# Gated delta heads on one Trainium2 core: norm factors folded into columns, 16x16 blocks inverted on VectorE

## The reference, cut to what matters

```python
qkv = jax.nn.silu(dwconv(pa[..., :3 * BR_W], conv_w))
q = l2norm(heads(qkv[..., :BR_W], H_A)) * (DK_A ** -0.5)
k = l2norm(heads(qkv[..., BR_W:2 * BR_W], H_A))
...
kb = k * beta
lower = jnp.where(strict, jnp.einsum('bhnid,bhnjd->bhnij', kb, k) * decay, 0.0)
rhs = jnp.concatenate([v * beta, kb * jnp.exp(gc)[..., None]], axis=-1)
sol = lax.linalg.triangular_solve(lower + jnp.eye(CHUNK, dtype=jnp.float32), rhs,
                                  left_side=True, lower=True, unit_diagonal=True)
...
o = rmsnorm(o_f + rev(o_b), norm_g)
y = merge_heads(o) * jax.nn.silu(z.astype(jnp.float32))
```

## Time and profile before

| | before |
|---|---|
| three runs, us | 2526.24, 2527.37, 2527.37 |
| the profiled execution, us | 2526.02 |
| its span, us | 2524.5 |
| mean granted TensorE clock | 0.997 |
| TensorE products busy, us | 2446.4 |
| VectorE / ScalarE / GpSimd busy, us | 1332.0 / 992.5 / 320.8 |

### The profile page before, as it was taken

The page is one execution under the profiler, slowest core; times in us unless marked ns, Lnnn a source line. Parts: engine busy times, 40 slices in busy tenths (PEclk is TensorE's granted clock), DMA queues, the critical chain, the costliest instruction groups (busy, mean ns, idle before and its releaser), DMA issues. The chain is left out here.

```text
span 2524.5 us, 56135 instructions
## 1 busy us (share of the span) xinstructions
PE 2446.4 (97%) x23072; PEld 2330.3 (92%) x23072; DVE 1332.0 (53%) x2347; ACT 992.5 (39%) x1908; POOL 320.8 (13%) x398
## 2 busy tenths in 40 slices
PE   7999999999999999999999999999999999999998
PEld 5889889999999999989988898899999999999898
DVE  5565653677333434663565656537773344356644
ACT  4555532333234424452365455323332353255422
POOL 1322201000012101110012222100000110011000
PEclk9999999999999999999999999999999999999999
DMA  7101114111234233124221110231113332222122
GB/s 270 46 31 40 31 37 149 43 43 51 101 106 106 81 108 99 57 63 147 76 92 46 31 40 23 69 133 34 51 50 87 88 91 83 77 68 82 55 99 84
DMA packets 55734, 193.86 MB, mean 77 GB/s; under 512 B 9080, under 2 KB 9246, under 8 KB 55376
## 3 DMA queue, kind: packets, MB, share of 16 engines
q1 hardware_dynamic: 40352, 147.34, 17.4%
q0 software_dynamic: 15152, 43.24, 6.3%
HBM read 177.97 MB, written 8.39 MB: 74 GB/s over the span
## 5 line engine op out<-in xcount | busy, mean ns | idle before, releaser
L734 PE MATMUL proj<-h_hi,w_hi 128*128 128x320 f32 x3072 | 739.5, 321 | 4.3 <-DVE h_lo L2171 2.9
L734 PE MATMUL proj<-h_lo,w_hi 128*128 128x320 f32 x3072 | 702.0, 309 | 0.0
L734 PE MATMUL proj<-h_hi,w_lo 128*128 128x320 f32 x3072 | 698.7, 309 | 1.3 <-issue 1.3
L2171 DVE TENSOR_TENSOR w_lo<-raw,w_hi 128x1024 fp32r<-128x1024 f32 x232 | 287.8, 1241 | 480.4 <-ACT w_hi L1573 479.6
L734 PEld LDWEIGHTS proj<-h_hi,w_hi 128*128 128x128 f32 x3072 | 504.1, 189 | 20.3 <-issue 5.9
L734 PEld LDWEIGHTS proj<-h_lo,w_hi 128*128 128x128 f32 x3072 | 514.8, 188 | 0.0
L734 PEld LDWEIGHTS proj<-h_hi,w_lo 128*128 128x128 f32 x3072 | 513.0, 188 | 1.6 <-issue 1.6
L734 PE MATMUL mix<-area 64*64 64x64 f32 (+6 forms) x8176 | 470.8, 236 | 11.8 <-issue 4.5
L734 PEld LDWEIGHTS mix<-area 64*64 64x64 f32 (+4 forms) x8176 | 405.0, 140 | 61.7 <-issue 36.5
L1573 ACT ACTIVATE w_hi<-raw 128x1024 fp32r<-128x1024 f32 x232 | 245.8, 1060 | 532.7 <-PE proj L734 329.7
L1573 ACT ACTIVATE area<-mix 128x256 f32<-128x256 f32 (+8 forms) x462 | 189.3, 433 | 632.9 <-PE mix L734 510.1
(11 more groups left out here) (304 smaller groups left out, 2653.7 us busy)
## 6 DMA issues: line engine op xcount, KB each, us to landing
raw<-in_w_in SPq DMA_DIRECT2D x128, 512.0 KB, 3.5
raw<-in_w_mb SPq DMA_DIRECT2D x96, 512.0 KB, 3.5
raw<-in_w_mod POOLq DMA_DIRECT2D x32, 512.0 KB, 4.7
area<-in_bias POOLq DMA_DIRECT2D x64, 128.0 KB, 4.6
raw<-in_w_out SPq DMA_DIRECT2D x16, 512.0 KB, 3.5
out_x<-area SPq DMA_DIRECT2D x10, 512.0 KB, 2.6
merged<-in_w_mod SPq DMA_DIRECT2D x8, 512.0 KB, 11.3
area<-area POOLq DMA_DIRECT2D x64, 64.0 KB, 1.9
```

The lines of the kernel that those rows point to most:

```text
L734: return T.matmul(out, l, r, start=start, stop=stop)
L2171: return V.tensor_tensor(out, a_, b_, op)
```

## The change

- **Norms.** Keys and queries stay unnormalised. Silu writes straight into `kq`, the operand of gram and scan. ScalarE squares it (`A_squared`), and ten products with one column of ones in front unit 3 give the sums; GpSimd takes the powers and multiplies them into the columns of beta (`A_front`); the queries' factor goes into the output norm. The 15 transposes of `kqn` and of q are gone, the front has 10 units with 20 transposes. Rv is now made by ScalarE.
- **Small blocks.** Levels 0 to 3 are gone. VectorE cuts the 16x16 diagonal blocks out (`A_decays`, `A_blocks`); five DMAs (three by SP, two by GpSimd) bring them to 40 partitions with a whole block in each; VectorE eliminates pivot by pivot, 28 small operations (`A_scaled`, `A_pivots`, `A_inverse`); five DMAs bring the inverses back, and VectorE and ScalarE spread them into X and Y (`A_spread`). Of the levels, one in halves, mid and last are left.
- **Order.** Front units 0 to 2 (the decays) of the next head stand among the first eighths of a head, units 3 to 9 in the scan; all engines' orders are rewritten. Blocks come right behind step 0 of the scan, pivots 1 to 3 behind step 3, pivots 4 to 8 and 9 to 14 before and behind w_lo of the next head's fourth unit.

```diff
@@ SP
+                def relay(h):
+                    sp.wait_ge(A_own.sem, A_own.at(layer, 3 * h + 2))
...
+                    for t in range(SP_TILES):
+                        blocks_in(sp, t, A_relay)
+                    sp.wait_ge(A_own.sem, A_own.at(layer, 3 * h + 3))
...
+                    for t in range(SP_TILES):
+                        inverses_back(sp, t, A_relay)
@@ GpSimd, A_front
+                    pool.wait_ge(A_fev.sem, A_fev.at(layer, FRONT * h + 4))
...
+                    P.tensor_tensor(roots, roots, neg_half[:, 0:10], ALU.pow)
...
+                    pt(A_head(1, h), A_head(1, h), both(rn_k(h))).then_inc(A_rn.sem, A_rn.step)
...
+                    pool.wait_ge(A_own.sem, A_own.at(layer, 3 * h + 1))
...
+                    pt(dec, decT, beta_sq.unsqueeze(3).to_broadcast([128, 2, TILES, 128])).then_inc(A_dm.sem, A_dm.step)
+                    pool.wait_ge(A_own.sem, A_own.at(layer, 3 * h + 2))
...
+                    for t in range(SP_TILES, TILES):
+                        blocks_in(pool, t, A_relay_pool)
@@ TensorE, A_front and A_levels
+                    elif u == 3:
+                        tr(o(0), kq[:, 0, tile(4)])
+                        for i in range(2):
+                            for t in range(TILES):
+                                last = mm(o(1)[:, 5 * i + t:5 * i + t + 1], A_c[:, i, tile(t)], ones[:, 0:1])
...
+                    fill(0, 1)
+                    if h < HEADS - 1:
+                        A_front(h + 1, 0)
+                        A_front(h + 1, 1)
+                    fill(1, 5)
+                    if h < HEADS - 1:
+                        A_front(h + 1, 2)
+                    fill(5, 17)
+                    A_level_q(h)
+                    fill(17, 18)
+                    A_level_d(h)
+                    if h:
+                        pe.wait_ge(proj_taken.sem, proj_taken.at(layer, u0 + 2))
+                        A_out(h - 1, psum_a[(u0 + 1) % 2])
+                    fill(18, 20)
+                    A_mid_q(h)
+                    fill(20, 21)
+                    A_mid_d(h)
+                    fill(21, 22)
+                    A_last_q(h)
+                    fill(22, 23)
+                    A_last_d(h)
+                    fill(23, 24)
@@ VectorE
+                def A_pivots(first, end):
+                    for p in range(first, end):
+                        n = 15 - p
+                        below = Z[:, p + 1:16, :, 0:p]
+                        tmp = Z_tmp[:, 0:2 * n * p].rearrange("q (i d c) -> q i d c", i=n, d=2)
+                        mul(tmp, Z[:, p + 1:16, :, p:p + 1].to_broadcast([40, n, 2, p]), Z[:, p, :, 0:p].unsqueeze(1).to_broadcast([40, n, 2, p]))
+                        fence()
+                        tt(below, below, tmp, ALU.subtract)
+                        fence()
...
                         if n == 0:
-                            A_squares(h + 1)
+                            A_blocks(h + 1)
                         elif n == 1:
-                            A_norms(h + 1)
-                        elif n == 2:
-                            A_normed(h + 1)
-                        elif n == 4:
                             A_lower(h + 1)
+                        elif n == 3:
+                            A_scaled(h + 1)
+                            A_pivots(1, 4)
```

More of the change, by code:

```diff
@@ L608, in _ @@
                 A_store(HEADS - 1)
[L609 removed]
+                A_o_root(HEADS - 1)
                 A_store_done(HEADS - 1)
@@ L1128, in part @@
                                 A_front(h + 1, u)
-                        if h < HEADS - 2:
+                        if h < HEADS - 2 and first < end:
+                            if h and first == 0:
+                                pe.wait_ge(A_ox.sem, A_ox.at(layer, h))
                             eighths(0, 4 * h + 8, first, end)
@@ L1133, in last_part @@
                         if h == HEADS - 1:
+                            if first <= 24 < end:
+                                pe.wait_ge(A_ox.sem, A_ox.at(layer, h))
                             eighths(0, 16, first, end)
@@ L2389, in update @@
+                def update(h):
+                    masks = [over(level[:, i, :].unsqueeze(1), TILES, 64) for i in range(2)]
                     for d in range(2):
-                        dve.wait_ge(A_d.sem, A_d.at(layer, e + (d + 1)))
+                        dve.wait_ge(A_d.sem, A_d.at(layer, 4 * h + (d + 1)))
                         held(dve)
-                        V.copy_predicated(X[:, d], masks[d], cols(1024 * d, 64) if lv else Q[:, d])
+                        V.copy_predicated(X[:, d], masks[d], cols(1024 * d, 64))
```

565 lines of the change are left out of this document (296 added, 269 removed).

## The result

| | before | the change |
|---|---|---|
| median, us | 2527.4 | 2546.3 (2540.2 to 2548.9) |
| ratio, 95% interval | | 1.007 (1.0057 to 1.0082) |
| profiled execution, us | 2526.0 | 2540.2 |
| its span, us | 2524.5 | 2538.7 |
| mean granted clock | 0.997 | 0.976 |

The forecast was 2531 with a range of 2498 to 2562. The time is 15 over it, 19 over before. The profiled execution of the change is the fastest of its four: the others took 2544.4 to 2548.9 us at a mean granted clock of 0.970 or 0.971.

What follows compares the result with a forecast made beforehand. TensorE, busy 97%, was taken to bound the kernel. Removed work and old pauses less new waits, with the layers' starts and end, gave −7.9; clock falls +12.8: 2526.0 − 7.9 + 12.8 = 2531 us, range 2498 to 2562.

Steps and rivals of the forecast that it cites:

- removed work turns into pauses: Leading case, whole kernel: work taken off TensorE returns as pauses of about the same length; 2515 to 2546 us, chance 0.45.
- What leaves TensorE: TensorE, branch A: delta groups of the dropped levels go, 52.5 us a layer, less 2.2 net for the changed front.
- The column products: Front, TensorE: ten one-column products a head, twenty instructions at 0.11 us each, +2.2 us; bounds nothing to 0.22 each.
- The new gate: Before the first kept level: TensorE waits for the 16x16 inverses to be spread, 6.6 to 6.9 us a head, 26.7 a layer.
- The relay back: Transfer returning the inverses before the spread: 1.9 us, bounds 1 and 6, covered by VectorE's convolution.
- Other new waits: TensorE per layer: output's transposes 1.9 × 3, mid and last levels 0.7 × 4, scan's start 6.2, third scan step 9.4 us.
- The scan's start: Scan start in three heads: TensorE waits for the third convolution, split, w_lo, value silu, gate and copy; 6.2 us.
- The layers' starts: Start of branch A: uncovered front work and waits for decay columns and square, +6.1 us in layer 0, +3.2 in layer 1.
- The third scan step: Scan: VectorE's blocks, slowed by meeting GpSimd's multiply, make this step 3.0 to 3.4 us late in three heads; 9.4 a layer.
- The clock: Behind the gate: one fall to half clock a head, about 3 us long, 1.6 lost, 8 × 1.6 = +12.8 us.
- B: Rival, faster: GpSimd's multiply misses the blocks, −18.8, and the clock stays full at the gate, −12.8; 2499 us, chance 0.32.
- C: Rival, slower: pivots at 0.5 us each lengthen the gate, +19, with second clock falls; 2556 or 2562 us, chance 0.23.

## Why the prediction was right

The sign of its sum (+4.9), its range and its leading case, *removed work turns into pauses*, came out; its point was 15 low (9 low against the profiled execution, 2540.2). The mechanism held for the gate; the number is near in part by luck, as the last steps show. By its own steps:

- **What leaves TensorE**, −100.6 for both layers: −100.0. The column products at 0.11 each: 2.29 for 20, so the row of 20 columns was the right one. Head 3's 14.05 should read 14.2 by its own terms, which changes nothing. The section "Wait — 56ns, not 53.3ns?" of the Trainium skill's page "TensorE: Matmul & The Clock Gate" gave an estimate of 1.2 for the twenty. The trace's 2.29 is above the floors stated there, so they are not what bounds here; weights of 128x128 come with each product, and 118 columns took nearly the same 2.39.
- **The new gate**, 6.6 a head in heads 0 to 2 and 6.9 in head 3: 6.0, 5.3, 5.5 and 5.7, 22.5 for 26.7 in layer 0, and 20.9 in layer 1. The chain's links were all there, pivots at 0.30. The chain ended at 24.5 (122.7 less the first eighth at 98.2) for 23.7. TensorE's idle time in heads 0 to 2 is less than forecast since the eighth and the level's first half, which stand between the pauses, ran at the low clock and filled part of them (3.2 us in head 0). In head 3 nothing stands between, and what made its 5.7 out of 6.9 was not looked into. The relay back was priced at 1.9; it took 4.5 in head 3, where the spread waits for it.
- **Other new waits.** The output's transposes, 1.9 × 3: 1.93 in three heads. The mid and last levels, 0.7 × 4: 3.0 in layer 0, with 1.10 of it the old pause of 1.09 in head 3, which the prediction had among those that go and which stayed. The scan's start, 6.2: 1.64 + 2.71 + 2.78 = 7.1. The layers' starts: in layer 0 5.2 for 5.4; in layer 1 2.2 and 3.5 for 2.4 and 3.7.
- **The third scan step**, 9.4 a layer, was the first step that failed. It measured 0.7, 0 and 2.9 in layer 0, 3.6, and 4.4 in layer 1. Price and mechanism of a meeting were read rightly from the earlier trace rows, and so was the race at the full clock: with 1.00 ahead of the blocks they start 0.2 us behind GpSimd's multiply, and layer 0 has 9.3. What was wrong was to price this wait and the clock apart. In the changed kernel's execution the clock was low ahead of all six blocks, ScalarE's copy of gram came 1.5 us behind GpSimd's start in head 0, and the blocks met only the multiply's end. Gate and third step make 21 of the 26 us by which idle time fell short.
- **The clock**, 1.6 once a head, +12.8, was the second, and in the other direction: 49.0 were lost, 3.8 times the term. I had counted one fall of 3 us a head, by the one fall that the trace of before shows in branch A. The changed kernel had falls of 3.4, 6.8 and 10.2 us, and behind three kinds of pause (gate, output or scan's start, layer's start), not behind the gate alone. The row was right for a single fall; it could not tell how many there would be or how long the clock stays low behind them. Filling the pauses took the stretches of 6.8 and 10.2 away (low-clock time 116 to 34 us), so they hang on the pauses; what makes one stretch longer than another stays open.
- The two misses, −26 of idle and +36 of clock, cancel but for 10 us, and that is luck in the size, if not wholly in the sign, since the low clock shortens the third step's wait. With the clock's miss alone the forecast's own sum would have stood at 2567, outside the range; with the idle time's alone at 2505, outside the forecast's own case (2515 to 2546). That case's bounds, by the way, fit a third of the pivots' ±19, which is 6, not the ±8 written there.
- **Rivals.** B needed the multiply to miss the blocks and the clock to stay full; the first came true for the most part and was worth 5 to 6 a layer, but because the second did not. C did not come (pivots 0.30), but its price, falls of the clock at more than one place a head, did.

## What to carry to other kernels

When a change takes work off the engine that bounds a kernel, list what that work covered and price the chain of the other engines up to the next gate link by link; here 100 us of products left, and the queues' order gave them back as 66 of pauses. Price a pause of TensorE twice, once for its length and once for the low clock behind it: here 66 us of pauses brought 49 of low clock. Do not price the clock apart from the races between other engines: a low clock delays what TensorE feeds into them. And look into each queue for work that stands behind a wait it doesn't need: four such moves (pivots and spread counted as one), with not one instruction removed, turned 0.7% slower into 2.3% faster.

## What the runs showed of the hardware that was not expected

- Filling pauses with useless products of 256 columns made a kernel faster by 23.5 us (0.9%), low-clock time 116 to 34 us.
- A granted clock of 0.50 came in stretches of about 3.4 us or two or three of that (3.4, 6.8, 10.2 in the windows).
- Five transfers, of 128 pieces of 136 bytes each on the way in and of 256 back, took on the way back 4.6 us from the inverse's end (115.2) to the spread's start in head 0 (119.8), where 64 KB by one queue took 1.9; in heads 1 and 2 VectorE's other work covered that. Of the 4.6, 2.0 are the three issues in a row on SP's queue.
- VectorE's two products of 40x256 elements and the small one behind them took 1.29 and 1.27 us together in heads 1 and 2 of layer 0, but in head 0, beside a 3.16 us multiply on GpSimd (98.97), the same three took 4.05. The meeting that cost 0.7 at head 0's blocks cost 2.8 there.
- Two kernels with the same order of work paid quite differently for the same race: the blocks took 1.98 to 2.98 us where the clock ahead was low, 3.93 or 3.94 where it was full.
